# Front, mixer tail and last expert tile of a two-layer hybrid model: work put in another order on VectorE, ScalarE and TensorE

## The reference

```python
h = rmsnorm(x, norm_mix[l]); z = h @ w_in[l]              # 1024 x 2304
z_rw, u_s5 = z[..., :RW_COLS], z[..., RW_COLS:]           # 1792 and 512 columns
vres = None if l == 0 else (rw_v0[l-1], rw_v1[l-1], rw_v2[l-1])
y_rw, v_first = rwkv7_mix(z_rw, h, ..., v_first, vres)    # gates, recurrence, group norm, bonus
y_s5 = s5_mix(u_s5, ...)                                  # complex linear recurrence, GLU, rmsnorm
x = x + concatenate([y_rw, y_s5]) @ w_out[l]
x = x + mem_cross_attention(rmsnorm(x, norm_xa[l]), rmsnorm(mem, norm_mem[l]), ...)
x = x + peer_ffn(rmsnorm(x, norm_ffn[l]), ...)            # 16384 experts, 8 heads x 16 chosen
```

## Time and profile before

| | us |
|---|---|
| median of three runs (lowest, highest) | 3953.64 (3948.75, 3964.07) |
| the profiled execution, whole | 3949.28 |
| its span, first to last instruction | 3947.6 |
| TensorE busy in the span | 3674.9 (93%) |
| VectorE busy | 2938.7 (74%) |
| ScalarE busy | 1352.4 (34%) |
| expert stage, layer 0 (730 to 2033) | 1303 |
| front, layer 0 (172 to 316) and layer 1 (2038 to 2208) | 144 and 170 |

### The profile page before, as it was taken

One profiled execution on the slowest core, in us unless ns is written; L12 is line 12 of the kernel. 1 busy time (PEld: TensorE's weight loads), 2 busy tenths in 40 slices (PEclk: granted clock), 3 DMA queues, 4 the chain that ended last, 5 costly groups with the idle time before them and its releaser, 6 DMA issues. The chain is left out here.

```text
span 3947.6 us, 69568 instructions
## 1 busy us (share of the span) xinstructions
PE 3674.9 (93%) x28586; PEld 3355.1 (85%) x28586; DVE 2938.7 (74%) x5404; ACT 1352.4 (34%) x2055; POOL 732.9 (19%) x592
## 2 busy tenths in 40 slices
PE   8798889899999989999989988989999999999998
PEld 5568767799999989999976776769999898999998
DVE  7566454588998977877766645458898897778876
ACT  3431233333334433333333123333333443333332
POOL 2000000022121132433410000002222112234431
PEclk9899899999999999999999998999999999999999
DMA  7721221387886899999942031227778688999995
GB/s 235 264 73 45 72 91 59 99 265 249 255 256 236 298 342 319 350 338 345 341 169 70 3 115 50 90 90 254 247 251 259 230 298 333 317 349 338 347 347 189
DMA packets 322781, 876.27 MB, mean 222 GB/s; under 512 B 29696, under 2 KB 158848, under 8 KB 315680
## 3 DMA queue, kind: packets, MB, share of 16 engines
q1 hardware_dynamic: 248736, 603.36, 45.1%
q0 software_dynamic: 73728, 268.47, 18.8%
HBM read 746.93 MB, written 124.78 MB: 221 GB/s over the span
## 5 line engine op out<-in xcount | busy, mean ns | idle before, releaser
L217 PE MATMUL peer_ps<-peer_h_high,tile_high 128*128 128x384 f32 (+1 forms) x2304 | 798.8, 347 | 63.0 <-ACT up_act L2342 23.0
L219 PE MATMUL peer_ps<-peer_h_high,tile_low 128*128 128x384 f32 (+1 forms) x2304 | 789.1, 342 | 0.0
L218 PE MATMUL peer_ps<-peer_h_low,tile_high 128*128 128x384 f32 (+1 forms) x2304 | 788.8, 342 | 0.0
L210 DVE TENSOR_TENSOR tile_low<-tile,tile_high 128x1024 fp32r<-128x1024 f32 x544 | 662.8, 1221 | 165.6 <-ACT tile_high L205 150.8
L217 PE MATMUL peer_ps<-gate_high,tile_high 128*128 128x384 f32 x2048 | 693.8, 339 | 29.5 <-DVE tile_low L210 29.3
L218 PE MATMUL peer_ps<-gate_low,tile_high 128*128 128x384 f32 x2048 | 691.3, 338 | 0.0
L219 PE MATMUL peer_ps<-gate_high,tile_low 128*128 128x384 f32 x2048 | 691.1, 337 | 0.0
L2222 POOL DMA_INDIRECT row<-in_peer_u_rows,row_at x256 | 314.5, 1229 | 1789.5 <-DVE row L2466 1064.1
L205 ACT ACTIVATE tile_high<-tile 128x1024 fp32r<-128x1024 f32 x544 | 571.0, 1050 | 32.2 <-DMA tile<-in_peer_u 31.8
L217 PEld LDWEIGHTS peer_ps<-peer_h_high,tile_high 128*128 128x128 f32 x2304 | 435.5, 189 | 90.5 <-issue 48.2
L2222 POOL DMA_INDIRECT row<-in_peer_v,row_at x256 | 391.9, 1531 | 636.5 <-DVE own_sum L2472 564.6
(11 more groups left out here) (480 smaller groups left out, 5200.1 us busy)
## 6 DMA issues: line engine op xcount, KB each, us to landing
tile<-in_peer_u SPq DMA_DIRECT2D x256, 512.0 KB, 4.6
tile<-in_peer_v SPq DMA_DIRECT2D x256, 512.0 KB, 6.3
gates<-gates_out SPq DMA_DIRECT2D x24, 2048.0 KB, 10.5
gates_in<-gates SPq DMA_DIRECT2D x32, 1536.0 KB, 14.5
acts<-up_act SPq DMA_DIRECT2D x240, 192.0 KB, 5.1
act_in<-acts SPq DMA_DIRECT2D x240, 192.0 KB, 6.4
in_w<-in_w_in SPq DMA_DIRECT2D x36, 512.0 KB, 3.3
tile<-in_peer_wq SPq DMA_DIRECT2D x32, 512.0 KB, 4.2
```

Source lines behind the costliest of these rows:

```text
L210: return dve.tensor_tensor(out, value, high.bitcast(F32), ALU.subtract)
L217: pe.matmul(out, wh, mh, start=first, stop=False)
L218: pe.matmul(out, wh, ml, start=False, stop=False)
L219: return pe.matmul(out, wl, mh, start=False, stop=last)
```

## The change

In the front, the products `ar[..., 1, :]` and `e` of each tile `t` move into a helper `receive`, called for tiles 2 and 3 at `j == 9` and for tiles 0 and 1 at `j == 10`, where `rk_made` is now given. The chunk ends are copied at `j == 9`, the product of `kk` and the gate moves from `j == 12` to 11, the scaling of `k` from 14 to 13, the mixing of `v` from 14 to 15. On ScalarE the exponential of `cum` goes behind the root and the widening. The later pair of `v2` products goes from tile 13 to tile 14, and its reading from `j == 14` to 15. In the tail, four of the eight turns go behind the centring, the scans are pulled apart, and `high(9)`, `low(9)` go ahead of the root and the reciprocal. In `peer`, the last tile completes bank after bank, and VectorE adds each one when it is complete.

```diff
@@ front, TensorE, ScalarE
-                if j in (11, 13) and layer:
+                if j in (11, 14) and layer:
                     pe.wait_ge(v1_taken.sem, v1_taken.at(1))
-                    for t in (j - 11, j - 10):
+                    for t in (0, 1) if j == 11 else (2, 3):
...
                 if j == 8:
-                    act.wait_ge(exps_made.sem, exps_made.at(2))
-                    act.activation(cum[:, :, :], cum[:, :, :], ACT.Exp, scale=-DECAY_SCALE).then_inc(exps_made.sem, 1)
                     act.wait_ge(kk_summed.sem, kk_summed.at(1))
                     act.activation(turned[:, :, :], sums, ACT.Sqrt).then_inc(kk_rooted.sem, 1)
...
+                    act.wait_ge(exps_made.sem, exps_made.at(2))
+                    act.activation(cum[:, :, :], cum[:, :, :], ACT.Exp, scale=-DECAY_SCALE).then_inc(exps_made.sem, 1)
-                if j in (12, 14) and layer:
+                if j in (12, 15) and layer:
@@ front, VectorE
+            def receive(some):
+                for t in some:
+                    last = dve.tensor_tensor(ar[:, t, :, 1, :], view(rT)[:, t], view(e[:, :, :])[:, t], ALU.mult)
+                link(last)
+                for t in some:
+                    last = dve.scalar_tensor_tensor(out=e[:, t, :], in0=rT[:, t, :], scalar=vec(pg, "rk")[:, t:t + 1],
+                                                    in1=kT[:, t, :], op0=ALU.mult, op1=ALU.mult)
+                link(last)
...
+                if j == 9:
+                    dve.wait_ge(exps_made.sem, exps_made.at(2))
+                    link(dve.tensor_copy(p_end[:, :, :], chunks(e[:, :, :])[:, :, :, CH - 1]))
+                    receive((2, 3))
                 if j == 10:
...
                     dve.sem_inc(kk_scaled.sem, 1)
+                    receive((0, 1))
+                    dve.sem_inc(rk_made.sem, 1)
...
-                if j == 14:
+                if j == 13:
                     link(dve.tensor_tensor(kT, kT, cum[:, :, :], ALU.mult))
+                if j == 15:
                     if layer:
                         dve.wait_ge(first_loaded.sem, first_loaded.at(16))
@@ tail, VectorE
-            for n in range(7):
+            for n in range(4):
+                turn(n)
+            for t in range(KH):
+                dve.wait_ge(mean_summed.sem, mean_summed.at(t + 1))
+                dve.scalar_tensor_tensor(out=y[:, t, :], in0=at_front[t][:, :], scalar=-1.0 / HEAD, in1=y[:, t, :],
+                                         op0=ALU.mult, op1=ALU.add).then_inc(centred.sem, 1)
+            for n in range(4, 7):
                 turn(n)
...
+            scan(0)
             dve.wait_ge(var_summed.sem, var_summed.at(1))
             dve.tensor_scalar(root[:, :, :], sums, 1.0 / HEAD, GN_EPS, ALU.mult, ALU.add).then_inc(varied.sem, 1)
+            link(scan(1))
+            dve.wait_ge(rooted.sem, rooted.at(1))
+            dve.reciprocal(root[:, :, :], root[:, :, :]).then_inc(turned.sem, 1)
...
             dve.tensor_scalar(rstd[:, :], ps[0][:, :], 1.0 / D_HALF, RMS_EPS, ALU.mult, ALU.add).then_inc(out_meaned.sem, 1)
+            low(9)
             dve.wait_ge(out_rooted.sem, out_rooted.at(1))
             link(dve.reciprocal(rstd[:, :], rstd[:, :]))
-            low(9)
@@ peer
+                if e == NKEY - 1:
+                    pe.wait_ge(row_used.sem, row_used.at(2 * ROWS))
+                for k in BANK_ORDER:
...
+                    if e == NKEY - 1:
+                        pe.matmul(ps[k][:, TD:T], own_sum[:, w], pg.c["ident"][:, :], start=True, stop=True).then_inc(own_turned.sem, 1)
...
-            dve.wait_ge(summed.sem, summed.at(UPS + NKEY))
-            dve.wait_ge(own_turned.sem, own_turned.at(1))
-            for k in range(KD):
+            for n, k in enumerate(BANK_ORDER):
+                dve.wait_ge(own_turned.sem, own_turned.at(n + 1))
                 last = dve.tensor_tensor(pg.xT[:, k, :], pg.xT[:, k, :], ps[k][:, :], ALU.add)
```

More of the change, by code:

```diff
@@ L568, in _ @@
                     for t in range(KH):
-                        dve.scalar_tensor_tensor(out=ar[:, t, :, 0, :], in0=view(kk[:, :, :])[:, t], scalar=-1.0,
-                                                 in1=view(lw[:, :, :])[:, t], op0=ALU.mult, op1=ALU.mult)
-                        last = dve.tensor_tensor(ar[:, t, :, 1, :], view(rT)[:, t], view(e[:, :, :])[:, t], ALU.mult)
+                        last = dve.scalar_tensor_tensor(out=ar[:, t, :, 0, :], in0=view(kk[:, :, :])[:, t], scalar=-1.0,
+                                                        in1=view(lw[:, :, :])[:, t], op0=ALU.mult, op1=ALU.mult)
                     link(last)
                     dve.sem_inc(heads_scaled.sem, 1)
+                    link(dve.tensor_tensor(av[:, :, :], kk[:, :, :], av[:, :, :], ALU.mult))
                 if j == 12:
[L575 to L581, removed]
                     link(dve.tensor_tensor(kk[:, :, :], av[:, :, :], cum[:, :, :], ALU.mult))
                     dve.sem_inc(b_made.sem, 1)
-                if j == 14:
+                if j == 13:
                     link(dve.tensor_tensor(kT, kT, cum[:, :, :], ALU.mult))
+                if j == 15:
                     if layer:
@@ L1132, in _ @@
             high(8)
+            high(9)
             act.wait_ge(out_meaned.sem, out_meaned.at(1))
             act.activation(rstd[:, :], rstd[:, :], ACT.Sqrt).then_inc(out_rooted.sem, 1)
-            high(9)
             high(10)
@@ L1173, in _ @@
             link(dve.tensor_tensor(rot[:, 1], sc[:, 1], sc[:, 0], ALU.subtract))
[L1174 to L1177, removed]
             pairs = lambda v: v.rearrange("p q n -> p (q n)")
-            for part in range(2):
-                last = dve.tensor_tensor_scan(pairs(sc[:, part]), pairs(keep), pairs(rot[:, part]), 0.0, ALU.mult, ALU.add)
-            link(last)
+            scan = lambda part: dve.tensor_tensor_scan(pairs(sc[:, part]), pairs(keep), pairs(rot[:, part]), 0.0, ALU.mult, ALU.add)
+            scan(0)
             dve.wait_ge(var_summed.sem, var_summed.at(1))
             dve.tensor_scalar(root[:, :, :], sums, 1.0 / HEAD, GN_EPS, ALU.mult, ALU.add).then_inc(varied.sem, 1)
+            link(scan(1))
+            dve.wait_ge(rooted.sem, rooted.at(1))
+            dve.reciprocal(root[:, :, :], root[:, :, :]).then_inc(turned.sem, 1)
             dve.tensor_tensor(tmp[:, 0], sc[:, 0], rotr, ALU.mult)
             link(dve.tensor_tensor(tmp[:, 1], sc[:, 1], roti, ALU.mult))
-            dve.wait_ge(rooted.sem, rooted.at(1))
-            dve.reciprocal(root[:, :, :], root[:, :, :]).then_inc(turned.sem, 1)
             dve.tensor_tensor(x[:, 0, :, 1:SN + 1], tmp[:, 0], tmp[:, 1], ALU.subtract)
@@ L2311, in _ @@
                                    (gh[m % NSPLIT][:, :], gl[m % NSPLIT][:, :]), e == 0, e == NKEY - 1)
-                last.then_inc(summed.sem, 1)
-            pe.wait_ge(row_used.sem, row_used.at(2 * ROWS))
-            for k in range(KD):
-                last = pe.matmul(ps[k][:, TD:T], own_sum[:, k * P:(k + 1) * P], pg.c["ident"][:, :], start=True, stop=True)
-            last.then_inc(own_turned.sem, 1)
+                    if e == NKEY - 1:
+                        pe.matmul(ps[k][:, TD:T], own_sum[:, w], pg.c["ident"][:, :], start=True, stop=True).then_inc(own_turned.sem, 1)
+                if e < NKEY - 1:
+                    last.then_inc(summed.sem, 1)
         @block.scalar
@@ L2648, in peer @@
         loaded[m % NRAW].passed(16)
[L2649 removed]
+    for s, n in ((high_made, UPS + NKEY), (low_made, UPS + NKEY), (summed, UPS + NKEY - 1), (taken, UPS), (keys_loaded, 16),
                  (scored, PH), (score_taken, 2 * PH), (searched, PH), (shifted, 1), (exped, 1), (found, 1), (flipped, TB - 1),
[L2651 removed]
+                 (flip_taken, TB - 1), (h_turned, 1), (h_flipped, 2), (row_used, 2 * ROWS), (rows_dotted, 1), (dots_gelued, 1), (own_turned, KD), (onehots_made, GROUPS), (spread, TD // 4), (gates_taken, TD // 4), (weighed, NKEY),
                  (added, 1), (squared, KD), (meaned, 1), (rooted, 1), (squares_summed, 1), (h_scaled, KD), (h_high_made, KD),
```

6 lines of the change are left out of this document (2 added, 4 removed).

## The result

The changed kernel takes 3922.94 us, the median of 18 runs (3917.17 to 3951.93), beside 3959.88 us for the kernel before in 18 runs on the same chip. The ratio on record is 0.9916, with a 95% interval of 0.9900 to 0.9931 (that of the two medians alone is 0.9907). Forecast were 3919 us and, by the sum, a ratio of 0.9918 (3916.7 / 3949.28).

The account below looks back on a forecast made before the run. TensorE, busy 93% of the span, was taken as the bound, its stands also costing clock. Fronts 10.2 and 12.1, `peer` 8.4, tail 1.7 and 0.2 sum to 32.6 us: 3916.7 or 3921.0, stated as 3919; range 3903 to 3936.

Parts of the forecast that it names:

- (a): Front: with the exponential of `cum` behind the root, root and widening come earlier; 1.1 us saved, 0.5 us of wait left.
- (b): Front, layer 0: products moved to `j == 9` and 10 fit VectorE's hole, so TensorE's 6.67 us wait goes.
- R1: Rival: VectorE takes over in both fronts, TensorE stands before tile 14; 4 to 6 us per layer, 3927 to 3933; chance 0.15.
- R3: Rival: the change doesn't do what it says, counts late another way; only `peer` and tail give 10 us, 3943; chance 0.05.
- (c): Front, layer 0: without the stand, the sums over `e` and tile 14 escape the slow clock; 2.4 us, bounds 0 to 2.4.
- Layer 1: Front, layer 1: the 7.68 us stand goes, VectorE sets the end, last take 12.1 us earlier; bounds 7.7 to 15.
- Peer: End of `peer`: one VectorE addition left behind the last matmul instead of eight; 4.2 us per layer, 8.4 in all.
- (d): Tail norm: centring after four turns shortens the wait for the squares; 1.4 us in layer 0, 0.3 in layer 1.
- (e): Tail: `low(9)` ahead of the reciprocal moves the wait from tile 9 to 10, 2.7 us there; 0.1 us per layer gained.
- R2: Rival: shorter tail stands give full clock; 3 us in (d), 1.5 in (e) per layer, 9 more, 3910; chance 0.12.
- R4: Rival: slower, as expert stages starting at another moment lengthen the 52.1 us of weight-tile waits; at double, 3971; chance 0.03.

Follow-up runs that it names:

- after: The changed kernel, all edits against the kernel before; its profiled execution takes 3921.36 us.
- filler: Kernel before plus seven products that nobody reads, put into TensorE's 6.67 us wait in layer 0's front; 3965.15 us in a single run.
- front_only: Kernel before with the front's edits alone; ratio 0.9945.
- after_again: The changed kernel as it is, run again beside later kernels; 3924.05 us, ratio 0.9912 to the kernel before.
- tail_early: Changed kernel with the rounding of half tiles 8 to 11 all ahead of the out norm; 3920.96 us, ratio 0.9891 to the kernel before.
- both_early: tail_early plus, in layer 1's front, `lw - v` and the chunk-end products of `kT` moved to `j == 14`; 3915.60 us, ratio 0.9892.
- peer_only: Kernel before with only the banks of the experts' output completed and added one by one; ratio 0.9965.
- tail_filler: Changed kernel plus three products that nobody reads per layer, ahead of the first two glu products; glu stage 45.04 and 45.00 us.
- best: both_early with the three products that nobody reads of tail_filler; 3909.98 us, ratio 0.9898 to the kernel before.

## Why the prediction was right, step by step

- **(a) Exponential behind the root.** 1.1 us forecast with 0.5 of wait left; 1.2 and 0.48 measured, the chain moved with it. The Trainium skill's rule ("ScalarE: Activation LUTs", "What ACT_TABLE_LOAD costs") of a drain of about 1.38 us more per switch did not show: 1.30 us lie between the start of the load and the root before, and 1.29 after.
- **(b) The products moved.** The 6.67 us went, and no wait stands ahead of tiles 12, 13 or 14 in either layer. R1 is out. (The times that the forecast gives for R1, at its upper end, and for R3 are 1 to 2 us higher than 3919 plus what they take away.)
- **(c) The clock.** 2.4 forecast, 2.26 in after and 2.2 by filler alone. The split was off: 1.8 was forecast for the eight passes and 0.6 for tile 14, and all 2.26 lie in the passes. They took 3.03 us to the next product, not the estimated 3.45, and the 0.6 rested on the 0.79-us row, which is there at full clock too. Layer 0: 10.2 forecast, 10.3 measured.
- **Layer 1.** 12.1 forecast, 12.2 in after, 12.3 in front_only, but 10.7 in after_again and 10.6 in tail_early, counted against before. That VectorE decides and not TensorE is shown twice, by its rows without a hole and by both_early, which gains by moving work of VectorE alone into its hole. TensorE's products there add up to 2178.4 and not to 2178.6, which changes nothing. Left out, and so put at nothing, was what TensorE's longer stand does to the clock behind it, about 2 us in the chunk stage.
- **Peer.** 4.2 per layer forecast, 4.25 at the row. peer_only's 13.8 us has an interval of 5 to 22, which holds 8.4. The stages of after are shorter by 6.8 and 5.9; the 4.3 us beyond the forecast are within their scatter and have no shown cause.
- **(d) Norm.** Mis-sized. Forecast 1.4 and 0.3. The stage gains 1.7 in layer 0; in layer 1 it takes 22.13 with the new order and 22.47 to 23.85 with the old in five profiles, so 0.3 to 1.7. And 0.1 to 1.6 per layer is lost in the glu products. That an earlier TensorE would find `lw_rounded` not ready and lose its clock was not in the forecast.
- **(e) low(9).** The wait moved to tile 10 with 2.72 us (2.7 forecast). The out stage averages 58.7 us with this edit in eight cases, 59.8 without it in twelve: 1.2 us a layer rather than 0.1, inside the bounds given. The clock makes this difference too. Over the out stage the granted clock is 0.94 in six of the eight, which take 58.2 to 58.5 us, and 0.91 in the other two (59.3 and 59.8, layer 0 of after the latter); without the edit it is 0.89 or 0.91 in eleven of twelve (59.4 to 60.4). Why it holds better with the edit is open.
- **R2** (a clock that gives more in the tail) priced 3 us in (d) and 1.5 in (e) per layer. In (d) the clock took instead; in (e) it gave 1.2 on average, near R2's price. **R3** is out. **R4**: the waits for expert tiles did not double (49.1 for 52.1 us), but the expert stage scatters by more than most terms of the sum. The intervals of the timed parts are some 8 us wide to each side, so the timing can't tell the smaller terms.

From the first mark of the front the profiles differ by 33.3 us, 32.6 forecast; the 5.3 us ahead of it are in untouched code. Fronts and the end of `peer` carried the sum, by the mechanism forecast. That it meets the measurement within 1 us is luck: in this profile the expert stages gave 4.3 us more than forecast and the tail 1.2 more, and the chunk stages took back 5.1 that the forecast did not have. About 2 of these 5.1 are the slow clock behind the stand in layer 1, and the rest is within the scatter of stages.

## What to carry to other kernels

Price a stand of TensorE by its length and by what runs behind it: the slow products cost 2.2 us after a stand of 6.67, 1.5 to 2.3 after one of 6.70, 0 to 0.2 after one of 2.0 to 2.4, and 0.1 to 1.6 after two short ones. When a chain is shortened so that TensorE arrives early at the next operand, look there first, for the gain may be lost to the clock. Products that nobody reads, put into a stand, are a cheap test of that, and here they kept the gain. And where VectorE has a hole just ahead of a chain that others wait for, pull the chain's independent members into it.

## What the runs showed of the hardware

The same instructions in the same order had a granted clock of 0.50 over 6 us of the glu products in after and of 0.76 in after_again, that is, the 1.2 GHz level lasted to 509.7 us in the one and to 506.1 in the other, behind stands of 1.66 and 1.44 us and of 1.23 and 1.45 us. The Trainium skill, "TensorE: Matmul & The Clock Gate", section "Part 1: The HAM clock gate (the "warmup" mystery)", says of the slow matmuls at a kernel's start that their count varies between runs of one kernel, and these rows agree, here in the middle of a kernel. Not expected was that three f32 products, six passes in 3.0 us, would remove this scatter in all four cases (two layers each in tail_filler and best), to 45.00 to 45.04 us.
